# Prompt attention: scaling the probabilities in place and transposing them plainly, instead of multiplying them by diagonal matrices

## What is computed

```
p_s = masked_softmax(s_s, causal);  o_s = p_s @ v_s
p_w = masked_softmax(s_w, causal);  o_w = p_w @ v_w
o   = g0 * o_c + g1 * o_s + g2 * o_w        (g: sigmoid gates, one per token, head and branch)
```

## Time and profile before

| | |
|---|---|
| median of three runs | 1206.3 us (1202.77 to 1208.32) |
| time of the profiled execution | 1201.1 us |
| its span in the trace | 1199.3 us |
| busy: TensorE, VectorE | 1123.1 us (94%), 690.5 us (58%) |
| busy: ScalarE, GpSimd | 332.5 us (28%), 304.8 us (25%) |
| mean granted TensorE clock | 0.963 of full speed |

### The profile page before, as it was taken

How to read it: one execution, slowest core, us unless ns; L and a number is a source line. 1 busy time by engine, 2 the same in 40 slices (tenths; PEclk the granted TensorE clock), 3 DMA queues, 4 the chain that set the end, 5 groups by cost and what they waited for, 6 DMA issues and landing times.

```text
span 1199.3 us, 19658 instructions
## 1 busy us (share of the span) xinstructions
PE 1123.1 (94%) x7798; PEld 885.4 (74%) x7798; DVE 690.5 (58%) x1496; ACT 332.5 (28%) x783; POOL 304.8 (25%) x346
## 2 busy tenths in 40 slices
PE   5899999877999799999999899999999999999995
PEld 3577777654677577877777686788887888778884
DVE  2753332688777478877775446554455454563245
ACT  2111110624665244544454213221111111000005
POOL 7200000163535677666662001000010000000000
PEclk8899999877999899999999999999999999999998
DMA  7733332155400776666663316121221221320202
GB/s 292 281 141 140 146 153 94 36 196 141 119 2 8 292 298 277 248 249 258 238 246 141 141 37 241 60 84 71 94 81 70 75 99 48 145 90 12 93 1 75
DMA packets 36842, 165.33 MB, mean 138 GB/s; under 512 B 4968, under 2 KB 15816, under 8 KB 27608
## 3 DMA queue, kind: packets, MB, share of 16 engines
q1 hardware_dynamic: 25304, 94.78, 21.5%
q0 software_dynamic: 11312, 69.38, 14.9%
q10 hardware_dynamic: 144, 0.04, 0.0%
HBM read 158.84 MB, written 9.24 MB: 140 GB/s over the span
## 4 chain that ended last, share of the span: by engine, by line
PE 83%; DVE 6%; DMA 4%; ACT 2%; POOL 2%; issue 1%; SPq 0%; ACTq 0%; DVEq 0%; POOLq 0%
PE PS L366 82%; DMA VX<-out_dram 2%; DMA ptc<-in_ptab_dram 1%; PE PS L1182 1%; POOL ptc L519 1%; ACT trunk L1829 1%; DVE w L2407 1%; DMA ringreg<-in_w_ada_dram 1%; DVE sreg L2455 1%; DVE sreg L2090 0%; DVE creg L2090 0%; PE PS L1255 0%; ACT ringreg L1643 0%; DMA ringreg<-in_w_o_dram 0%; DVE ringreg L2115 0%
## 5 line engine op out<-in xcount | busy, mean ns | idle before, releaser
L366 PE MATMUL PS<-mixreg,w 128*128 128x272 f32 (+1 forms) x596 | 139.7, 386 | 9.9 <-DVE mixreg L2085 4.2
L366 PE MATMUL PS<-creg,ringreg 128*128 128x272 f32 (+1 forms) x564 | 144.2, 400 | 3.5 <-ACT creg L1522 2.8
L366 PE MATMUL PS<-mixreg,ringreg 128*128 128x272 f32 (+1 forms) x532 | 132.3, 402 | 5.5 <-DMA ringreg<-in_w_o_dram 4.4
L366 PEld LDWEIGHTS PS<-mixreg,w 128*128 128x128 f32 x596 | 110.5, 195 | 32.0 <-issue 8.3
L366 PEld LDWEIGHTS PS<-creg,ringreg 128*128 128x128 f32 (+1 forms) x564 | 104.6, 188 | 33.1 <-issue 9.8
L366 PEld LDWEIGHTS PS<-mixreg,ringreg 128*128 128x128 f32 (+1 forms) x532 | 100.2, 191 | 28.0 <-DMA ringreg<-in_w_o_dram 4.8
L366 PE MATMUL PS<-zreg 128*32 128x128 f32 (+4 forms) x832 | 107.2, 327 | 9.1 <-POOL zreg L667 4.8
L366 PE MATMUL PS<-creg,w 128*128 128x256 f32 (+1 forms) x432 | 106.7, 392 | 0.0
L366 PEld LDWEIGHTS PS<-creg,w 128*128 128x128 f32 x432 | 81.8, 193 | 17.6 <-issue 4.3
L366 PEld LDWEIGHTS PS<-zreg 128*32 128x32 f32 (+2 forms) x832 | 73.0, 142 | 23.0 <-issue 6.0
L366 PE MATMUL PS<-mixreg,sreg 128*128 128x272 f32 x352 | 87.3, 395 | 0.0
(11 more groups left out here) (392 smaller groups left out, 1873.7 us busy)
## 6 DMA issues: line engine op xcount, KB each, us to landing
ringreg<-in_w_ada_dram SPq DMA_DIRECT2D x24, 1024.0 KB, 7.1
ringreg<-in_w_f_dram SPq DMA_DIRECT2D x22, 1024.0 KB, 4.8
ringreg<-in_w_in_dram SPq DMA_DIRECT2D x11, 1024.0 KB, 4.8
ringreg<-in_w_f_dram SPq DMA_DIRECT2D x8, 704.0 KB, 4.2
creg<-in_w_f_dram SPq DMA_DIRECT2D x8, 704.0 KB, 6.8
sreg<-in_win_dram SPq DMA_DIRECT2D x8, 512.0 KB
ringreg<-in_w_o_dram SPq DMA_DIRECT2D x4, 1024.0 KB, 8.0
out_dram<-in_win_dram SPq DMA_DIRECT2D x1, 4064.0 KB
```

Source lines behind the costliest of these rows:

```text
L366: return nc.tensor.matmul(o, lhsT, rhs, start=start, stop=stop, **kw)
```

## The change

The product of the reciprocal and the gate is no longer made by VectorE. GpSimd scales the probabilities themselves, in place in `PB[t % 3]`, by two numbers per token in one instruction: the reciprocal row sum, and the gate read from `GT`. That is (j + 1) x 128 columns for each branch, where a diagonal matrix had 128. TensorE turns the scaled blocks with plain transposes, which have the identity as the moving operand. The diagonal buffers go. GpSimd's wait for the transposes of tile t-2 and VectorE's wait for GpSimd go; ScalarE's exponentials get a wait for GpSimd's scaling of tile t-2.

```diff
-        DG = [RS[:, 6400 + b * 2 * P:6400 + (b + 1) * 2 * P].rearrange("p (q i) -> p q i", q=2) for b in range(2)]
...
             for t in range(NTL):
                 pool.wait_ge(sem("nsa_scale"), t + 1)
-                if t >= 2:
-                    pool.wait_ge(sem("nsa_pt"), 2 * (t - 1))
+                j, g = t // 2 % TT, t % 2
+                gate = RANK + 6 * (t // 8) + 3 * g + 1
                 for q in range(2):
-                    nc.gpsimd.tensor_scalar(DG[t % 2][:, q, :], ident[:, :], pst[:, t % 2, 3, q:q + 1], None, ALU.mult).then_inc(sem("nsa_p"), 1)
+                    p = PB[t % 3][:, q * LP:q * LP + (j + 1) * P]
+                    nc.gpsimd.tensor_scalar(p, p, pst[:, g, 2, q:q + 1], GT[:, j, gate + q:gate + q + 1], ALU.mult, ALU.mult).then_inc(sem("nsa_p"), 1)
                 if t < 8:
                     cmp_load(0, (t,))
...
                 for q in range(2):
                     pe.wait_ge(sem("nsa_p"), 2 * t + q + 1)
                     for k in range(j + 1):
-                        last = matmul(PS[:, 6 + q, k * P:(k + 1) * P], pb[:, q * LP + k * P:q * LP + (k + 1) * P], DG[t % 2][:, q, :], True, True)
+                        last = nc.tensor.transpose(PS[:, 6 + q, k * P:(k + 1) * P], pb[:, q * LP + k * P:q * LP + (k + 1) * P], ident[:, :])
                     last.then_inc(sem("nsa_pt"), 1)
...
                 if t >= 3:
                     act.wait_ge(sem("nsa_pt"), 2 * (t - 2))
+                if t >= 2:
+                    act.wait_ge(sem("nsa_p"), 2 * (t - 1))
                 act.wait_ge(sem("nsa_max"), t + 1)
...
-                j, g = t // 2 % TT, t % 2
-                st = pst[:, g]
-                gate = RANK + 6 * (t // 8) + 3 * g + 1
+                st = pst[:, t % 2]
                 dve.wait_ge(sem("nsa_exp"), 2 * (t + 1))
-                if t >= 2:
-                    dve.wait_ge(sem("nsa_p"), 2 * (t - 1))
-                link(nc.vector.reciprocal(st[:, 2, :], st[:, 2, :]))
-                nc.vector.tensor_tensor(st[:, 3, :], st[:, 2, :], GT[:, j, gate:gate + 2], ALU.mult).then_inc(sem("nsa_scale"), 1)
+                nc.vector.reciprocal(st[:, 2, :], st[:, 2, :]).then_inc(sem("nsa_scale"), 1)
```

## The result

The changed kernel takes 1186.46 us in the median of four runs (1186.13 to 1192.5), against 1204.73 for the kernel before on the same chips. The ratio is 0.9863, with a 95% interval of 0.9835 to 0.9891: 1.4% faster. The forecast was 1209.4 with a range from 1199 to 1227, so both the direction and the range were wrong.

A forecast was written before the change was run, and what follows sets the result against it. TensorE was taken to set the pace, busy 22.38 of 23.00 us a group. Pieces 27.5 + 45.2 + 19.4 + 3.1 + 4.8 = 100.0 us against 97.05, 3 us more: 1206.3 becomes 1209.4, range 1199 to 1227.

The forecast's parts named there:

- TensorE's part: In the stage's transposes, one pass replaces two: TensorE gives up 5.0 us and needs 17.4 us a group.
- VectorE's part: Between reciprocals, the gate product goes, 0.20 us: a round of 2.44 us becomes 2.24.
- GpSimd's part: In-place scaling with two scalars costs 0.28 us plus 2.51 ns a column, 17.3 us a group instead of 9.4.
- The lower bound: GpSimd's scaling at 1.42 ns a column at most, 0.73 us for 512 columns, taken from the mask selection.
- The second rival: GpSimd's scaling at the low bound, 1.42 ns a column: stage 82.5 us, 14.5 less, 1192 us; chance 0.12.
- The pieces of the kernel before: Stage cut at GpSimd scalings: 26.93 us for eight tiles, 46.16 for sixteen, 15.82 to tile 31, 8.14 after.
- The waits: Across the stage's engines, three waits go or move; the longer scaling delays TensorE, repaying its 5.0 us with GpSimd's 7.9.
- the walk: Scaling starts stepped through a group of eight tiles, taking the latest condition each time: next group at 22.6 us.
- the three conditions: A scaling starts after the previous scaling, after VectorE's round, and after scaling plus TensorE-VectorE chain from two tiles earlier.
- The lock: VectorE's negated maximum may wait for GpSimd's running scaling to finish: 0 to 0.4 us a group.
- The first rival: GpSimd's second multiply is not free, 3.76 ns a column: stage 118 us, 21 more, 1227 us; chance 0.21.
- The third: With less to multiply, TensorE's clock falls from 2.4 to 1.2 GHz: 35 us more, 1241 us; chance 0.03.

The follow-up runs named there:

- two-scalar diagonal: The kernel before, with GpSimd building the diagonal by reciprocal and gate in one instruction and VectorE's product dropped: 1200.64 us, ratio 0.9984.
- identity products: The changed kernel, with two-pass products with the identity in place of the plain transposes: 1201.16 us, ratio 0.9994.
- the row of 5743 ns: Adding 1.0 to TH, 2176 columns, far from the stage; the changed kernel with a multiply by 1.0 added there: 1192.64 us once, then 1186.16, ratio 0.9861.
- the kernel that really has those prices: The changed kernel, but VectorE again multiplies reciprocal and gate, and GpSimd scales in place with one operation: 1210.62 us, ratio 1.0063.

## Why the prediction was wrong

**What bounds the kernel now** was right: TensorE. The experiments with the two-scalar diagonal and the identity products show it from two sides: with TensorE's passes as they were, neither moved the time of the kernel before.

**TensorE's part** was right in kind and a little large: 4.1 us a group instead of 5.0. The forecast took the spacing of nine transposes in a row (0.11 us). In the stage a tile has one run for each branch, and the eight at 344.30 took 1.28 us, where that spacing with 0.27 us behind the last gives 1.04 (7 x 0.11 + 0.27). The rest was not taken apart.

**VectorE's part** was right: a round with a reduction of 0.96 us took 2.22 us (333.38 to 335.60), and 2.24 had been worked out.

```profile
333.38 0.16 DVE L2180 RECIPROCAL ringreg<-ringreg 128x2 f32<-128x2 f32 x1
...
334.53 0.96 DVE L2173 TENSOR_REDUCE ringreg<-PS 128x2 f32<-128x768 f32 x1
...
335.60 0.16 DVE L2180 RECIPROCAL ringreg<-ringreg 128x2 f32<-128x2 f32 x1
```

**GpSimd's part** is the step that failed: "I take 2.51: it is the same operation, measured at both ends of the widths, and a loop this slow per column looks like one that handles the second operation anyway." It is not the same operation. With a second operation it took 0.84 ns a column, a third; the row of 5743 ns fell to 2006 when it got one. Both rows had one operation, and a line can be drawn through any two points, so it said nothing about the case at hand. The Trainium skill's sentence (GPSIMD Engine Reference, 4.1 Engine selection), one-input work at roughly line rate, was set aside because of that row. The form with two operations agrees with it, at 0.84 ns a column (VectorE's reduction in the earlier trace rows takes 1.05, 0.54 us for 512 columns). It does not hold for the form with one, at 2.51 ns.

**The lower bound** of the same step was badly drawn: it was to lie below every likely price, and the measured one, 446 to 769 ns, lies below its 0.60 us at 128 columns and a little above its 0.73 us at 512. The second rival was this case, with 1192 us and 14.5 less; the measured stage is 15.7 less. That the sum came so near is in part luck: its first group of 23 us took 20.77, and its steady groups of 18.5 took 17.70 and 19.21. But it got 0.12, and the range reached only half way to it, to 1199. A range that leaves out a bound has to say which row excludes that bound, and the row that was to do so had another form.

**The pieces of the kernel before** were misread by a tile, as the table shows. The forecast's times are sums of their own and stay, but two comparisons fail: 19.4 us from tile 24 to tile 31 is 0.7 less than before and not "3.6 more", and the 3 us that the forecast adds come from the first eight tiles alone, 27.5 against 22.70.

**The waits** held roughly for the forecast's prices. They give 100.0 us for the stage, and the kernel that really has those prices took 102.8, by pieces 27.20, 45.81, 21.49 and 8.29. That kernel keeps VectorE's product; with its 0.2 us in the second and third condition the walk gives 23.4 us a group and 20.2 from tile 24 to tile 31, and the profile has 23.23 and 21.49. The 1.3 us over the 20.2 lie in the step behind tile 24, where the clock was low: 4.47 us (366.50 to 370.97), and 3.14 a group earlier (343.26 to 346.40). Behind tile 31 VectorE was not sooner than GpSimd: the load waited 0.40 us for it.

With the measured prices (P = 0.89, 1.11, 1.32 and 1.54 us) the three conditions no longer set the pace. The walk gives 18.6 us for a group and 17.8 when it is carried into the next, while the profile has 17.70 and then 19.21. In the longer group TensorE works 18.23 us and waits 0.71 for ScalarE's copies, which none of the conditions contains. ScalarE's new wait cost nothing that shows: no wait of ScalarE's in the stage is put down to GpSimd.

**The lock** does not matter after the change: the negated maximum never took longer than 270 ns. In the kernel with one operation it took up to 786 ns, but only six of the 32 took over 0.2 us.

**The first rival**, a second multiply that costs more, is excluded: the second multiply makes the instruction cheaper. **The third**, the clock, did not come in the change: from 297.30 to the load it stands at 1.00. But the forecast's own case was not free of it: in the kernel with the forecast's prices, where TensorE waits for the scaling, the clock did fall, twice, for 6.8 and 3.4 us. What brings it down was not tried. The rule of the Trainium skill on transposes (TensorE: Matmul & The Clock Gate, Part 4: PE-mode transpose), that the full clock does not engage for them, does not agree with this trace: in the earlier trace rows the granted clock rose under plain transposes alone, and after the change it stays at 1.00 with 40 of them among 155 instructions.

## What to carry to other kernels

A price is that of a form, not of an operation's name: before two rows are joined by a line, compare the number of operations and operands, and where the new form has no row, keep both ends in the range. Where GpSimd multiplies many columns by one number, or adds one to them, in f32, give the instruction a second operation, even a multiply by 1.0, and read its row again; the time changes only where something waits for it, as the row of 2006 ns shows. Before a stage is cut into pieces, count the rows. Where one engine fills 97% of a stage, little counts but what shortens that engine's own instructions (here 13.0 of 13.7 us); once it is shorter, the next engine counts as well. A transpose made by a product with a scaled identity costs TensorE twice the passes, and the scale is cheaper anywhere else that has room.

## What the runs showed of the hardware that was not expected

GpSimd's tensor_scalar in f32 took 0.28 us plus 2.51 ns a column with one operation and 0.27 to 0.34 us plus 0.83 to 0.84 ns a column with two, in place, from 128 to 512 columns; at 2176 columns it was 5743 against 2006 ns. Out of place, at 128 columns, it was 602 against 451 ns. What the engine does differently in the two cases, no run shows.

TensorE's granted clock fell to 0.50 for 3.4 us or more inside this stage in three kernels, one with single-operation scalings and two with another order of the query blocks. Shortly before each fall TensorE had waited 0.7 to 0.9 us for a scaling, but most waits of that length brought no fall. In all other profiles it stood at 1.00 from tile 8 to the load.
